# Grouping a mixture's experts by their token counts (128, 64 and 32 rows), summing in PSUM, and making every extra round conditional

## What is computed

```python
h = modulate(rms_norm_2(x, g_pre_ffn), shift_f, scale_f)      # 256 x 1024
logits = h @ w_router + b_router                              # 256 x 32 experts
top_val, top_idx = top_k(logits, 4);  gates = softmax(top_val)
# for each expert e, for the tokens that chose it:
hg = xblk @ w_gu[e] + b_gu[e]                                 # 1024 -> 2048
x_glu = minimum(hg[:, :1024], 7);  x_lin = clip(hg[:, 1024:], -7, 7)
act = x_glu * sigmoid(1.702 * x_glu) * (x_lin + 1)
y[token] += gate * (act @ w_down[e] + b_down[e])              # 1024 -> 1024
x = x + gate_f * rms_norm_2(y, g_post_ffn)
```

## Time and profile before

| | us |
|---|---|
| median of three runs | 2367.19 |
| lowest, highest | 2366.9, 2371.65 |
| profiled execution, its own time | 2368.39 |
| its span, first to last instruction | 2366.6 |
| TensorE busy in the span | 2272.3 (96%) |
| VectorE, ScalarE, GpSimd busy | 673.7, 381.2, 135.3 |
| bytes read from HBM | 597.29 MB, mean 253 GB/s |

### The profile page before, as it was taken

One profiled execution on the slowest core, in us unless ns is written; L12 is line 12 of the kernel. 1 busy time (PEld: TensorE's weight loads), 2 busy tenths in 40 slices (PEclk: granted clock), 3 DMA queues, 4 the chain that ended last, 5 costly groups with the idle time before them and its releaser, 6 DMA issues.

```text
span 2366.6 us, 25898 instructions
## 1 busy us (share of the span) xinstructions
PE 2272.3 (96%) x10937; PEld 1477.7 (62%) x10937; DVE 673.7 (28%) x1325; ACT 381.2 (16%) x686; POOL 135.3 (6%) x191
## 2 busy tenths in 40 slices
PE   8999999999999999999999999999999999999995
PEld 6887788888878888888777733333334433333332
DVE  3344422334264132335244411111111111111112
ACT  3321122100024121000232400000000000000001
POOL 0013300000000000000000000000000000000000
PEclk9999999999999999999999999999999999999998
DMA  6220062333542335347533189999999899999994
GB/s 240 106 73 36 2 232 107 143 133 142 227 178 107 142 142 214 134 159 288 201 119 113 68 370 428 426 428 428 425 428 418 366 379 427 427 427 427 427 427 178
DMA packets 43323, 600.08 MB, mean 254 GB/s; under 512 B 5232, under 2 KB 5504, under 8 KB 6688
## 3 DMA queue, kind: packets, MB, share of 16 engines
q1 hardware_dynamic: 43200, 598.36, 62.0%
HBM read 597.29 MB, written 1.05 MB: 253 GB/s over the span
## 4 chain that ended last, share of the span: by engine, by line
PE 84%; DMA 11%; DVE 2%; ACT 1%; issue 0%; SPq 0%; PEldq 0%; DVEq 0%; ACTq 0%
PE pb L402 83%; DMA ring<-in_gu 6%; DMA arena<-in_dne 5%; PE pb L412 2%; DMA arena<-in_dn 1%; DVE arena L319 0%; DVE arena L304 0%; ACT arena L363 0%; ACT xs L363 0%; ACT xt L363 0%; DVE ring L319 0%; DMA col<-in_cols 0%; SPq L540 0%; PEldq L3032 0%; DVE xt L304 0%
## 5 line engine op out<-in xcount | busy, mean ns | idle before, releaser
L402 PE MATMUL pb<-arena 128*64 128x512 f32 (+8 forms) x2316 | 681.9, 451 | 11.7 <-DMA ring<-in_gu 8.8
L402 PE MATMUL pb<-ring,arena 128*64 128x512 f32 x1648 | 480.9, 595 | 1.7 <-DMA ring<-in_dne 1.6
L402 PE MATMUL pb<-xt,ring 128*128 128x256 f32 (+3 forms) x1808 | 402.5, 383 | 3.8 <-DVE xt L319 3.6
L402 PEld LDWEIGHTS pb<-arena 128*64 128x64 f32 (+4 forms) x2316 | 274.4, 157 | 186.2 <-issue 168.3
L402 PEld LDWEIGHTS pb<-xt,ring 128*128 128x128 f32 (+3 forms) x1808 | 339.2, 189 | 62.4 <-issue 7.6
L402 PE MATMUL pb<-kv,arena 128*64 128x512 f32 (+2 forms) x592 | 265.2, 604 | 35.1 <-DMA arena<-in_dne 34.4
L402 PEld LDWEIGHTS pb<-ring,arena 128*64 128x64 f32 x1648 | 153.0, 137 | 202.5 <-issue 202.5
L402 PEld LDWEIGHTS pb<-kv,arena 128*64 128x64 f32 (+1 forms) x592 | 88.3, 154 | 196.8 <-issue 194.3
L369 ACT ACTIVATE arena<-pb 128x512 f32<-128x512 f32 (+2 forms) x131 | 74.4, 568 | 614.6 <-PE pb L412 415.3
L304 DVE TENSOR_TENSOR mix<-pb,mix 128x512 f32<-128x512 f32 x68 | 47.1, 692 | 429.9 <-PE pb L402 429.6
L363 ACT ACTIVATE arena<-arena 128x512 f32<-128x512 f32 (+4 forms) x151 | 86.5, 573 | 296.8 <-DVE arena L319 269.1
(11 more groups left out here) (180 smaller groups left out, 1954.2 us busy)
## 6 DMA issues: line engine op xcount, KB each, us to landing
ring<-in_gu SPq DMA_DIRECT2D x67, 2048.0 KB, 18.9
arena<-in_gu SPq DMA_DIRECT2D x48, 2048.0 KB, 16.6
ring<-in_dne SPq DMA_DIRECT2D x32, 2048.0 KB, 13.8
arena<-in_dne SPq DMA_DIRECT2D x18, 2048.0 KB, 17.5
kv<-in_gu SPq DMA_DIRECT2D x17, 2048.0 KB, 15.5
kv<-in_dne SPq DMA_DIRECT2D x16, 2048.0 KB, 13.0
ring<-in_up SPq DMA_DIRECT2D x13, 2048.0 KB, 7.9
ring<-in_ada SPq DMA_DIRECT2D x9, 2048.0 KB, 8.2
```

Source lines behind the costliest of these rows:

```text
L402: r = self.e.matmul(out, lhsT, rhs, start=start, stop=stop, skip_group_check=True)
```

## The change

- A fixed order becomes one by count. Experts 0 to 3 stay as pairs (`e0`, `e1`). The other 28 are ranked on chip by their token count: VectorE counts for each how many are larger (`KEY`, `PERM`), TensorE permutes ranks, gates and room (`sorted_p`, six small matmuls), VectorE takes them over (`sorted_v`) and writes the order into `NI`.
- The two largest are jobs of one expert over 128 rows (`w0`, `w1`), the next 18 are pairs over 64 (`p0` to `p8`), the last eight are two jobs of four over 32 rows each (`q0`, `q1`). The order is `e0 e1 p0 p1 q0 w0 p2 p3 p4 p5 w1 p6 p7 p8 q1`: 15 jobs in place of 17, 32 experts in place of 32 and a round. A step of a four is 64 records of shape 128*32.
- The weights of all but the first four experts are fetched by an address computed from `NI`, once SP has waited for `mo.order`.
- All 15 rounds lie behind conditions; the count is loaded by each engine in the sixth job (`COUNT_AT`), the engines wait for each other only inside round 0, and `s_join` counts TensorE alone.
- Nine places: `xt` and `mix` become the ends of `arena`, the biases `BG` and the two `xgs` buffers lie over constants that are no longer read, and there is one `ats`, `ys` and `sg` in place of two. So eight places are in the ring, and a ninth (`once`) is used for one unit alone, the first expert's `gu00`, which is issued after `mo.t11`, when `xt` is free.
- `Y` is no more in SBUF: PSUM banks 4 to 7 hold it, `biases_p` starts them and every `scatter_p` adds to them; `scatter_v` is gone. All other products share banks 0 to 3. The order of the first steps changes: `biases_p` and `sorted_p` run in the first job's `second()`, `back_p` in the third job's. The two bias matmuls of a half now stand together ahead of its first step, over 32 rows, and wait for both of its banks.
- The end: ScalarE squares the four banks while VectorE multiplies them by the gain, in turns; one pass per half then gives the output, which is written in two halves. The table of functions for logarithm and exponential is loaded before the last two copies.

```diff
...
+FIXED = 4
+CAPS = [128] * 2 + [64] * 18 + [32] * 8 + [64] * FIXED
...
+    def once(self, k, name, piece, *marks):
+
+        self.m.put("slot " + name, k)
+        self.wait_ge(*marks)
+        self.ge(self.order[-FLIGHT])
+        sem = self.sems(f"slot{k}")
+        at, rows, src = piece
+        if self.e is not None:
+            self.e.dma_start(self.slots[k][0:rows, at:], src).then_inc(sem, 16)
+        self.order.append((sem, 16))
+        self.m.put("load " + name, (sem, 16))
...
+        Lane.slots += [AR.t[:, EXTRA - SLOT:EXTRA], AR.t[:, EXTRA - 2 * SLOT:EXTRA - SLOT]]
+        Lane.slots += [ALL[:, 2 * D + TOP:], ALL[:, 0:SLOT]]
+        IN_KV, IN_EXTRA, IN_MOE, IN_MOE2, IN_MIX, ONCE = 3, 4, 5, 6, 7, 8
...
+        xgs = [DEAD[:, n * D:(n + 1) * D].rearrange("p (c t) -> p c t", c=8) for n in range(2)]
+        YP = DEAD.rearrange("p (i d) -> p i d", i=2)
+        ys = MT_[:, 0:1024]
...
         def biases_p(P):
+
             P.wait_ge("load b_down16")
             for i, half in TURNS:
-                b = P.tile(f"mo.y{i}{half}")
+                b = P.occupy(f"mo.y{i}{half}", Y_BANK + 2 * i + half)
                 P.wait_ge("free mo.gtt")
-                P.mm(b, GTT[0:32, i * 128:(i + 1) * 128], BDOWN[:, half * 512:half * 512 + 512], True, True,
+                P.mm(b, GTT[0:32, i * 128:(i + 1) * 128], BDOWN[:, half * 512:half * 512 + 512], True, False,
                      sig=f"mo.y{i}{half}")
...
+            V.tt(KEY, b[:, 64:96], cst["tie"], ADD)
+            V.stt(JUNK, KEY, 1.0, cst["id4"], MUL, MUL, accum=KC)
+            V.stt(JUNK, KEY, KC, ones[:, 0:32], ALU.is_gt, MUL, accum=RC1)
+            V.ts(PERM, cst["row32"], RC1, None, ALU.is_equal, None)
+            V.stt(JUNK, PERM, 1.0, cst["cap"], MUL, MUL, accum=CAPC)
+            V.copy(CAPB, CAPC.to_broadcast([128, 128]))
+            V.mark("mo.perm")
...
+        def sorted_v(V):
+            b = V.tile("mo.pm")
+            V.copy(PT2, b[:, 0:128])
+            V.mark("mo.pt")
+            V.copy(NI[0:1, 16:48], b[0:1, 160:192])
+            V.mark("mo.order")
+            V.copy(CAP, b[:, 128:160])
+            V.free("mo.pm")
...
+        def route_g(lane, n):
+            width = 128 // len(GROUPS[n])
+            rank, gate = (RK, GT) if n[0] == "e" else (RKP, GTP)
+            for g, e in enumerate(GROUPS[n]):
+                maps_g(lane, slice(g * width, (g + 1) * width), [rank[:, i, e:e + 1] for i in range(2)],
+                       [gate[:, i, e:e + 1] for i in range(2)])
...
         def up_p(P, n, q, k, count, sel, between=None):
+            b = [P.tile(f"{n}.h{k}{gl}", hold=True) for gl in range(2)]
+            P.wait_ge("load bg16", f"free {n}.s", f"{n}.gm", "mo.s0")
+            for gl in range(2):
+                rows = slice((k * 2 + gl) * 32, (k * 2 + gl) * 32 + 32)
+                P.mm(b[gl], sel[rows, :], BG[rows, :], True, False, sig=f"{n}.b{k}" if gl else None)
             for gl in range(2):
                 if gl and between is not None:
                     between()
-                b = P.tile(f"{n}.h{k}{gl}", hold=True)
-                P.wait_ge("load bg16", f"free {n}.s", f"{n}.gm", "mo.s0")
-                P.mm(b, sel, BG[:, (k * 2 + gl) * 512:(k * 2 + gl) * 512 + 512], True, False)
-                expand_p(P, b, xgs[q], units_of(n, f"gu{k}{gl}", count), False, f"{n}.h{k}{gl}")
+                expand_p(P, b[gl], xgs[q], units_of(n, f"gu{k}{gl}", count), False, f"{n}.h{k}{gl}")
...
         def scatter_p(P, n, q):
+            P.wait_ge(f"free {n}.d1")
             for i, half in TURNS:
-                b = P.tile(f"{n}.z{i}{half}")
-                P.wait_ge(f"free {n}.d1")
-                P.mm(b, SCT[q][:, i * 128:(i + 1) * 128], ys[q][:, half * 512:half * 512 + 512], True, True,
-                     sig=f"{n}.z{i}{half}")
-
-        def scatter_v(V, n):
-            for i, half in TURNS:
-                b = V.tile(f"{n}.z{i}{half}")
-                o = Y[:, i, half * 512:half * 512 + 512]
-                V.tt(o, b, o, ADD)
-                V.free(f"{n}.z{i}{half}")
-
-        JOBS = [f"e{p}" for p in range(PAIRS // 2)] + ["r0"] + [f"e{p}" for p in range(PAIRS // 2, PAIRS)]
-        PICK_AT = 3
-
-        def experts_of(n):
-
-            return (2 * int(n[1:]), 2 * int(n[1:]) + 1) if n[0] == "e" else None
-
-        def width_of(n):
-            return 2 if n[0] == "e" else 1
+                P.mm(P.banks[Y_BANK + 2 * i + half], SCT[q][:, i * 128:(i + 1) * 128],
+                     ys[:, half * 512:half * 512 + 512], False, True, sig=f"{n}.z" if i + half == 2 else None)
+
+
+
+
+        GROUPS = {f"e{n}": (2 * n, 2 * n + 1) for n in range(FIXED // 2)}
+        GROUPS.update({f"w{n}": (n,) for n in range(2)})
+        GROUPS.update({f"p{n}": (2 * n + 2, 2 * n + 3) for n in range(9)})
+        GROUPS.update({f"q{n}": tuple(range(4 * n + 20, 4 * n + 24)) for n in range(2)})
+        JOBS = "e0 e1 p0 p1 q0 w0 p2 p3 p4 p5 w1 p6 p7 p8 q1".split()
+        REST_AT, COUNT_AT = 2, 6
...
                 def second():
+                    if at == 0:
+                        biases_p(P)
+                        sorted_p(P)
                     turn_act_p(P, n, 0)
+                    if at == REST_AT:
+                        back_p(P, HT, "mo.r")
                     if late is not None:
                         scatter_p(P, late, 1 - q)
                     if at + 1 < len(JOBS):
                         route_p(P, 1 - q, JOBS[at + 1])
-                    if at == PICK_AT:
-                        pick_p(P, 0)
-
-                if n == "r0":
-                    P.wait_ge("free r0.oh")
-                up_p(P, n, q, 0, width_of(n), sel, first)
+                    if at == COUNT_AT:
+                        count_of(P)
+
+                up_p(P, n, q, 0, len(GROUPS[n]), sel, first)
...
+            S.table(LNEXP)
+            turn_act_s(S, JOBS[-1], 1)
+            contract_s(S, JOBS[-1])
...
+        def count_of(lane):
+
+            lane.wait_ge("mo.ni")
+            if lane.e is not None:
+                counts[lane.kind] = lane.e.value_load(NI[0:1, 15:16], min_val=0, max_val=15)
...
         def rounds(lane, body):
 
 
-            lane.joined("moe.end", LANES)
             lane.begin("round")
-            count = None
-            if lane.e is not None:
-                lane.wait_ge("mo.ni")
-                count = lane.e.value_load(NI[0:1, 15:16], min_val=0, max_val=15)
+            before = dict(lane.seen)
             with ExitStack() as asked:
-                for r in range(1, ROUNDS):
+                for r in range(ROUNDS):
                     if lane.e is not None:
-                        asked.enter_context(lane.e.If(count > r))
+                        asked.enter_context(lane.e.If(counts[lane.kind] > r))
+                    if r == 0:
+                        lane.joined("moe.end", LANES)
                     body(r)
                     lane.ge(lane.last)
-            if lane.e is not None:
-                lane.e.sem_inc(sems("s_join"), 1)
-            lane.last = None
+            lane.last, lane.seen = None, before
             lane.begin("post")
...
+        def end_s(S):
+            summed(S)
+            for n, (i, half) in enumerate(TURNS):
+                if i:
+                    S.wait_ge(f"end.y{i}{half}")
+                S.act(XS[:, i, half * 512:half * 512 + 512], S.banks[Y_BANK + n], ACT.Square,
+                      accum=SQS[:, 2 * half + i:2 * half + i + 1])
+                S.mark(f"end.q{i}{half}")
+            S.wait_ge("end.s")
+            S.act(STMP, SS, ACT.Ln, scale=1.0 / D, bias=EPSC)
+            S.act(RS, STMP, ACT.Exp, scale=-0.5)
+            S.mark("end.e")
+
+        def end_v(V):
+            summed(V)
+            for i, half in ((1, 0), (1, 1), (0, 0), (0, 1)):
+                o = slice(half * 512, half * 512 + 512)
+                if i == 0:
+                    V.wait_ge(f"end.q{i}{half}")
+                V.tt(YP[:, i, o], V.banks[Y_BANK + 2 * i + half], PG[:, o], MUL)
+                V.mark(f"end.y{i}{half}")
+            V.wait_ge("end.q11")
+            V.tt(SS, SQS[:, 0:2], SQS[:, 2:4], ADD)
+            V.mark("end.s")
+            V.ts(STQ, SS, 1.0 / D, EPS, MUL, ADD)
+            V.wait_ge("end.e")
+            V.tt(STMP, STQ, RS, MUL)
+            V.stt(STMP, STMP, -0.5, RS, MUL, MUL)
+            V.stt(RS, STMP, 1.5, RS, ADD, MUL)
+            for i in range(2):
+                V.stt(HTOK[:, i, :], YP[:, i, :], RS[:, i:i + 1], HTOK[:, i, :], MUL, ADD)
+                V.mark(f"post.h{i}")
...
+                for g, e in enumerate(F.experts):
+                    src = dram[what][bass.ds(e * per + u, 1)].rearrange("a p n -> (a p) n")
+                    F.load(f"{n}.{name}.{g}", (0, 128, src), ordered=n[0] != "r")
...
+            def first_loads(u):
+
+                for g, e in enumerate(GROUPS[JOBS[0]]):
+                    if (u, g) == (2, 0):
+                        F.join(IN_MOE, "hg.o1")
```

(20 more changed lines are left out.)

284 lines of the change are left out of this document (146 added, 138 removed).

## The result

The changed kernel takes 2311.81 us (median of four runs, 2309.14 to 2312.95) against 2368.24 for the kernel before (2366.9 to 2371.65): a ratio of 0.975, 95% interval 0.9734 to 0.9771, 56.4 us less. The forecast was 2309.

A forecast was written before the change was run, and what follows sets the result against it. The expert stage was taken as a weight stream at its limit, TensorE close behind. Round 29.5, dip 8.4, start 10.8 and end 9.8 gave 58.5 us off the profiled 2368.39, hence 2309 at the median; range 2290 to 2333.

The forecast's parts named there:

- The round: Expert stage: no round is left, so six units of weights at 4.91 us go, 29.5 us less.
- The dip: Queue's idle time at round 0, 16.5 us before: 8.1 left at `w1`, so 8.4 us less; bounds 0 and 16.5.
- The account: Count of ring places held when a job's last step ends; gave 16.0 us for round 0's dip against 16.5 seen.
- The limit of 7.35: Units that eight ring places can hold before the queue loses time, one place staying free only in part (0.65).
- The start: Nine units loaded early, first step near 1354.9 in place of 1359.9: 10.8 us less; bounds 0 and 21.
- the prediction's own signs of being wrong: Rounds run, a four's step over 19.6 us, under 420 GB/s outside `w1` and the first job, first step not earlier.
- The end: Last byte to end of span: 26.8 us in place of 36.6, 9.8 us less; bounds 14 and 2 less.
- Fours, addresses, additions: A four's step takes 7.1 us, hidden up to 19.6; computed addresses cost 0; scatter additions in PSUM cost 0.
- Rival 2: Fours' weight loads stand between matmuls: 14.6 us a step, 7.5 more in the last, 5 at `w0`: 2321; chance 0.07.
- rival 4: A round is left behind the last job, some 65 us less 3 of cover: 2371; chance 0.03.
- rival 3: Fours in `q0` and `q1` do not run side by side: 27.4 us a step, some 110 us: 2418; chance 0.02.
- Rival 1: The lead is worth more, queue starts without a pause and `w1` costs nothing: 10+8 more, 2291; chance 0.09.

The follow-up runs named there:

- run 1: The kernel before with round 0 taken out of its jobs, leaving out ten tokens of expert 27: 2326.15 us, ratio 0.981.
- run 8: The changed kernel with the eight smallest experts as four pairs over 64 rows in place of two fours: 2313.72 us, ratio 0.977.
- run 2: The changed kernel with seven places in the ring in place of eight: 2322.48 us, ratio 0.980.
- run 12: The changed kernel unchanged, run again in the third batch: 2310.45 us, ratio 0.975.
- run 4: The changed kernel unchanged, run again in the first batch: 2314.03 us.
- run 6: The changed kernel with each four's step in two halves of two experts: 2322.24 us, ratio 0.981.
- run 9: The changed kernel with both jobs of one expert moved right ahead of the fours: 2304.11 us, ratio 0.972.
- run 7: The changed kernel without jobs of one expert, ten pairs instead, one conditional round after the last job: 2375.31 us, ratio 1.003.
- run 5: The changed kernel with a four's matmuls issued one expert after another instead of alternating: 2399.78 us, ratio 1.013.
- run 11: The changed kernel with jobs of one expert right ahead of the fours and biases added in the second job: 2301.22 us, ratio 0.971.

## Why the prediction was right

**The round, 29.5 us: right.** 192 issues, six units fewer, and run 1 gives it back together with the dip: 45.9 by the profiles and 44.4 by the medians, against 29.5 + 16.5 = 46.0.

**The dip, 8.1 us left by the forecast, 6.1 measured.** What was mis-sized is the length of TensorE's jobs. The account gave `w1`'s job and the next one 54.85 us each, in which 22.4 units land and 18 are asked, a surplus of 4.4. In the trace the last steps of `p5`, `w1` and `p6` end at 1949.8, 2002.7 and 2056.1: 53.15 us each, 21.65 units, a surplus of 3.65. The 4.6 held ahead of them were 4.5. So 4.5 + 3.65 - 7.35 = 0.8 units, 4 us, where 4.3 were lost. The limit of 7.35 stands. A ring of eight does fill up to 8, as the first job shows, but the load issued into the empty queue then took 7.7 us to land and not 4.9, and these 2.8 us are 0.57 of a unit, near the forecast's 0.65. The same sum gives 3.9 and 5.7 us at the single jobs of run 8 (measured 5.3 and 5.7; 4.5 and 4.85 were held ahead of them) and 8.8 at `w1` of run 2 with seven places (measured 9.1). And `w0` after a four was put at 6.9 held, came to 7.5 and lost 1.8 us: its lead was taken 0.6 units too low. Why wasn't tried. For round 0 of the kernel before, the same reading (53.4 and 53.7 us) gives 4.6 + 3.8 - 5.35 = 3.05 units, 15.0 us, against 16.5 seen. So the account is good to 1 or 2 us, and the prediction's agreement within half a microsecond was partly luck.

**The start, 10.8 forecast, the term that was most wrong.** The last load landed at 2285.9; the last one before, issued at 2312.2, landed 19.5 us later, at 2331.7. That is 45.8 us less, of which 29.5 are the round and 16.5 - 6.1 = 10.4 the dips. 5.9 are left for the start. The landings show it directly: the 17th unit landed at 1419.9 and before at 1425.6, 5.7 earlier. In run 12, with the same code, it landed at 1416.9, 8.7 earlier. The step that failed is an unspoken one, that the mixture is reached when it was before. The logits start at 1335.05 in the trace of before, and in those of the changed kernel at 1340.68, 1337.34 (run 4) and 1337.41 (run 12); at a lower clock (0.80 granted from 1340 to 1346) they then take up to a us more. From the transposes on, the steps went as forecast: 15.7 us to the first step in the profile above and 16.2 in run 12 (forecast 1354.9 - 1339.08 = 15.8), and 39.8 and 40.0 from there to the end of the first job's last step (forecast 1394 - 1354.9 = 39.1). So that end comes at 1401.2 and 1398.2, 7.2 and 4.2 us late, and since the ring is full by then, each of them is a us without loads: 5.7 + 7.2 = 12.9, and 8.7 + 4.2 = 12.9. Runs 6 and 9 have the same code up to there and were not late: their first jobs ended at 1394.8 and 1394.7, and their 17th units landed 12.2 and 12.3 us earlier than before's. The places are therefore worth some 12 us, a little over the forecast, to a kernel that reaches the mixture in time; the profiled execution was not one. Two of the prediction's own signs of being wrong came up in it: a first step that is not earlier (1361.40 against 1359.90), and GB/s under 420 at `w0` (403).

**The end, 9.8 forecast, 10.3 measured.** From the landing of the last load to the end it is 24.6 us, not 26.8. But before it was 34.9, not 36.6: the prediction read the last byte off a window that ends at 2330. The two errors, 2.2 and 1.7, nearly cancel. The step took 8.6 in place of 10.1: the low clock lasted 3 us here and not the 6 of the forecast, and cost 1.6. The branch left 0.06 of the 1.0 put down for it. The rest met its terms: squares, logarithm, root and steps 4.5 for 4.6 (2299.10 to 2303.57), two passes 2.6, output 4.3 for 4.0. The Trainium skill's rule on taken branches (Runtime: NRT & Kernel Launch, Instruction fetch mechanics) agrees in kind with run 7's 3.33 us. In the changed kernel, where the scatter's 3.7 us were still queued, 0.06 us of it stand on the path.

**The sum.** 29.5 + 10.4 + 5.9 + 10.3 = 56.1. It closes because the start is the remainder, but the 17th unit gives 5.7 for it by itself. The forecast's 58.5 had the start 4.9 too high, the dip 2.0 and the end 0.5 too low. That the total came within 2.4 us is partly luck: with the mixture reached in time, as in runs 6 and 9, the start would have been some 6 us larger and the time below the forecast.

**Fours, addresses, additions: right.** The twelve steps of fours took 8.5 to 9.9 us, since each starts at the lower clock after a wait. Behind that their groups of four records follow each other by 0.43 us, which would be 6.9 us for sixteen:

```profile
2272.19 0.59 PE L409 MATMUL pb<-arena 128*32 128x512 f32 x1
2272.21 0.60 PE L409 MATMUL pb<-ring,arena 128*32 128x512 f32 x2
2272.22 0.59 PE L409 MATMUL pb<-kv,arena 128*32 128x512 f32 x1
2272.62 0.59 PE L409 MATMUL pb<-arena 128*32 128x512 f32 x1
```

No weight load shows: four of them belong to each group, 0.11 us each here, and if they stood between the matmuls the groups would be 0.87 apart. The rule of the Trainium skill (TensorE: Matmul & The Clock Gate, Part 3, The mechanism), that a weight load overlaps only where row groups differ, holds no better for 32 columns than for 64. What the fours bring is another matter: by run 8 some 5 us.

**The rivals.** Rival 2's price was met by run 6, rival 4's by run 7 (63 against 62), rival 3's place and point by run 5, whose step was 22.6 and not 27.4, so +88 and not +110 (the terms written down for that rival, 38, 39 less 15, 38, 7.8 and 20, add up to 128). Rival 1's mechanism is real, a lead that costs nothing at the single jobs, but the change doesn't reach it; run 11, at 2301, goes half of the way.

**Left open.** When the mixture is reached varies from execution to execution: in the twelve traces of kernels with the change the logits start between 1333.6 (run 5) and 1340.7, four of them earlier than in the trace of before, 1335.05. So a late arrival does not come with the change as such. Nor can the earlier loads of weights be its main cause: in the profile of the result the first unit of an expert was issued at 1234.0, before at 1229.9, so 4.1 of the 5.6 us were there ahead of it. What it is stays open; in each batch of four the logits start later with the number of the run (1334.5 to 1337.3, 1333.6 to 1336.8, 1334.1 to 1337.4). The table load and the branch were not undone one by one: their part in the end is read from the timeline alone. The sums in PSUM were not undone by themselves either.

## What to carry to other kernels

Where a stream of weights is the limit, count the places held at the end of each job: a job that works longer than it loads costs time only if its surplus fills the ring, so put a job that loads longer than it works right behind it. Saving engine time in such a stage is worth little but where the ring is full and behind the last byte. Compare stretches between two landings, not only whole times: the part ahead of the stage varied here by 7 us, more than most of the terms. Work that has to happen once belongs in a job with slack, not in the first one, whose places the queue is waiting for.

## What the runs showed of the hardware

- With up to four loads of 2 MB under way, landings follow each other by 4.9 us (427 GB/s). When all eight places held landed units the queue moved 0 GB/s (1398.9 to 1401.3), and the load issued into it then took 7.7 us to land. So a ring that fills costs the time it stands still and 2.8 us more.
- Matmuls of 32 columns from four experts run side by side, four in the time of one, only when they are issued in turns. In series a step of 64 took 22.6 us, not 27.4, and 20.7 from start to start: at each border a few run beside the next expert's.
- After a wait for weights TensorE starts at the lower of its clocks, and the time to the higher one differs even for the same shape: about 3 us in the last step (1.07 us a matmul, then 0.61; 9.8 us idle ahead of it), 5.8 us in the step before it (2266.4 to 2272.2, granted clock 0.50; 6.9 us idle ahead of it), and some 6 us behind the row of before.
